# Modulation rows of the first block in two column halves, and part of a later row summed on VectorE

## The reference, cut to what matters

```python
mod = silu_c @ w_ada[l] + b_ada[l]
shift_m, scale_m, gate_m, shift_f, scale_f, gate_f = jnp.split(mod, N_MOD, axis=-1)

h = modulate(rmsnorm(x, g_norm_mix[l]), shift_m, scale_m)   # h * (1 + scale) + shift
proj = h @ w_in[l]
...
x = x + gate_m[:, None, :] * mix
```

## Time and profile before

| | us |
|---|---|
| median of 3 runs | 2786.18 |
| the runs | 2789.58, 2786.18, 2762.64 |
| the profiled execution | 2768.54 |
| its span, first to last instruction | 2766.9 |
| what lies around the span | 1.64 |
| PE busy | 2641.7 (95%) |
| DVE busy | 1923.6 (70%) |
| ACT busy | 1112.8 (40%) |

### The profile page before, as it was taken

One profiled execution on the slowest core, in us unless ns is written; L12 is line 12 of the kernel. 1 busy time (PEld: TensorE's weight loads), 2 busy tenths in 40 slices (PEclk: granted clock), 3 DMA queues, 4 the chain that ended last, 5 costly groups with the idle time before them and its releaser, 6 DMA issues.

```text
span 2766.9 us, 53993 instructions
## 1 busy us (share of the span) xinstructions
PE 2641.7 (95%) x21560; PEld 2477.9 (90%) x21560; DVE 1923.6 (70%) x2016; ACT 1112.8 (40%) x1270; POOL 171.6 (6%) x281
## 2 busy tenths in 40 slices
PE   6999998899999999998998999999979999999998
PEld 2676777799999999997998989999959999999997
DVE  1446576777787776878867888888767466575664
ACT  1334443434343443444333444444434344343443
POOL 5000000100000000100000000001010000000000
PEclk8899999899999999998999999999979999999998
DMA  9997756678888887885766665568737676666753
GB/s 367 345 354 262 218 187 202 197 265 289 278 290 302 285 288 243 298 280 188 246 222 191 220 214 174 164 221 282 270 115 238 204 232 214 204 229 206 230 196 113
DMA packets 301892, 658.80 MB, mean 238 GB/s; under 512 B 30688, under 2 KB 37176, under 8 KB 299320
## 3 DMA queue, kind: packets, MB, share of 16 engines
q1 hardware_dynamic: 269496, 539.35, 57.9%
q0 software_dynamic: 32256, 117.45, 13.1%
HBM read 654.62 MB, written 2.10 MB: 237 GB/s over the span
## 4 chain that ended last, share of the span: by engine, by line
PE 85%; DVE 7%; DMA 3%; ACT 2%; issue 2%; SPq 0%; DVEq 0%; ACTq 0%; POOLq 0%
PE ps L1789 25%; PE ps L1790 24%; PE ps L1791 24%; DVE lo L1008 2%; PE ps L1834 1%; DMA proj<-in_w_ada 1%; PE ps L1836 1%; PE ps L1835 1%; ACT hi L606 1%; PE ps L1995 1%; DVE work L1020 1%; DMA ada_ring<-in_w_ada 1%; PE ps L1948 0%; PE ps L2253 0%; DMA raw<-in_w_in 0%
## 5 line engine op out<-in xcount | busy, mean ns | idle before, releaser
L1008 DVE TENSOR_TENSOR lo<-raw,hi 128x1024 fp32r<-128x1024 f32 x868 | 1049.2, 1222 | 648.5 <-ACT hi L606 646.5
L606 ACT ACTIVATE hi<-raw 128x1024 fp32r<-128x1024 f32 x868 | 911.3, 1059 | 1272.5 <-PE ps L1791 988.6
L1789 PE MATMUL ps<-acts,hi 128*128 128x256 f32 x4432 | 1249.4, 282 | 26.3 <-DVE lo L1008 12.0
L1790 PE MATMUL ps<-acts,hi 128*128 128x256 f32 x4432 | 1236.3, 279 | 0.0
L1791 PE MATMUL ps<-acts,lo 128*128 128x256 f32 x4432 | 1236.1, 279 | 0.0
L1789 PEld LDWEIGHTS ps<-acts,hi 128*128 128x128 f32 x4432 | 841.2, 190 | 67.8 <-issue 46.6
L1790 PEld LDWEIGHTS ps<-acts,hi 128*128 128x128 f32 x4432 | 840.4, 190 | 1.4 <-issue 0.8
L1791 PEld LDWEIGHTS ps<-acts,lo 128*128 128x128 f32 x4432 | 839.3, 189 | 0.4
L1789 PE MATMUL ps<-f_acts,hi 128*128 128x256 f32 x2048 | 566.7, 277 | 0.8 <-DVE lo L1008 0.8
L1790 PE MATMUL ps<-f_acts,hi 128*128 128x256 f32 x2048 | 565.8, 276 | 0.0
L1791 PE MATMUL ps<-f_acts,lo 128*128 128x256 f32 x2048 | 565.8, 276 | 0.0
(11 more groups left out here) (259 smaller groups left out, 1324.3 us busy)
## 6 DMA issues: line engine op xcount, KB each, us to landing
raw<-in_w_ff SPq DMA_DIRECT2D x512, 512.0 KB, 4.7
raw<-in_w_in SPq DMA_DIRECT2D x232, 512.0 KB, 4.6
ada_ring<-in_w_ada POOLq DMA_DIRECT2D x224, 512.0 KB, 5.0
proj<-in_w_ada SPq DMA_DIRECT2D x32, 1024.0 KB, 8.3
proj<-in_w_ada SPq DMA_DIRECT2D x40, 512.0 KB, 5.6
ada_ring<-in_w_ada SPq DMA_DIRECT2D x34, 512.0 KB, 5.9
raw<-in_w_out SPq DMA_DIRECT2D x32, 512.0 KB, 5.0
raw<-in_w_o SPq DMA_DIRECT2D x32, 512.0 KB, 5.2
```

Source lines behind the costliest of these rows:

```text
L606: nc.scalar.activation(hi[n % SPLIT][:, :], raw[n % RAW][:, :], ACT.Copy).then_inc(hi_ready, 1)
L1008: V.tensor_tensor(lo[n % SPLIT][:, :], raw[n % RAW][:, :], hi[n % SPLIT][:, :].bitcast(F32), ALU.subtract)\
L1789: M(out, h, right[:, 0:S], start=start, stop=False)
L1790: M(out, h, right[:, S:2 * S], start=False, stop=False)
```

## The change

Four things are changed.

1. Scale and shift are made in two column halves. Block 0 takes 8 double-row tiles of scale columns 0 to 1023 and 8 of shift columns 0 to 1023; block 1 the same for columns 1024 to 2047, now 16 tiles between chunks 1 and 9 (`tiles_after`). There are four `turn_block` steps in place of three.
2. The first 8 row tiles of segment 2 become 16 halves of 512 KB. DVE multiplies each with its silu column and adds it to one of two accumulators (`ada_halves`), after the split of the chunk that `half_lo` names: twelve behind chunks 16 to 24, four behind chunks 28 to 31. Each is loaded behind the chunk two later than that (`ada_half`). PE adds the accumulators up once, after chunk 31 (`sum_halves`). The other 24 tiles of segments 2 and 3 stay pairs on PE, now after chunks 33 to 62; before, 16 of the 32 stood after chunks 12 to 30. The row of segment 2 is finished one group later.
3. In the last group ahead of a norm DVE writes the output first and splits the next chunk behind it (`out_first`; for the first output projection by its own loop).
4. Pieces of the three big later norms are 1, 1, 2, 4, 4 and 4 tiles, and PE waits for them tile by tile.

The diff, cut to its core:

```diff
-PAIRS, EARLY, LEAD = 3, 2, 3
+PAIRS, LEAD = 3, 3
+HALVES = KT
...
+        half_tiles = pair_tiles[0] + pair_tiles[2]
+        half_landed = [sem(f"half_landed{i}") for i in range(len(half_tiles))]
+        half_used = sem("half_used")
...
-        pair_after = {(PER_BLOCK + 5 * p // 4 if p < KT else FIRST + 12 + 26 * (p - KT) // 15): p for p in range(2 * KT)}
-        tile_after = {j: j - 2 for j in range(2, 10)}
+        half_lo = (16, 17, 18, 19, 19, 20, 21, 21, 22, 23, 23, 24, 28, 29, 30, 31)
+        pair_after = {(33 + 8 * (p - 8) // 7 if p < KT else 43 + 19 * (p - KT) // 15): p for p in range(HALVES // ADA, 2 * KT)}
+        BLOCK_ROWS = 2 * BLOCKS
+        TILES = 2 * KT // BLOCKS
+        tiles_after = {1: (0,), 2: (1, 2), 3: (3,), 4: (4, 5), 5: (6,), 6: (7, 8), 7: (9, 10), 8: (11, 12), 9: (13, 14, 15)}
...
-            return [(0, 2), (2, 4), (4, 8), (8, 12), (12, 16)] if tiles == KT else [(0, tiles)]
+            if tiles < KT:
+                return [(0, tiles)]
+            return [(0, 1), (1, 2), (2, 4), (4, 8), (8, 12), (12, 16)]
...
-            def scale_tile(k):
-
-                start_slot(k, w_ada[0][k * P:(k + 1) * P, D:2 * D].rearrange("(t p) n -> p t n", p=P))
-
-            def shift_tile(b, m):
-
-                rows = w_ada[0][2 * P * m:2 * P * (m + 1), b * 2 * NC:(b + 1) * 2 * NC]
-                start_slot(KT + 8 * b + m, rows.rearrange("(t p) n -> p t n", p=P))
+            def block_tile(b, m):
+
+                col = (m // 8 == 0) * D + b * 2 * NC
+                rows = w_ada[0][2 * P * (m % 8):2 * P * (m % 8 + 1), col:col + 2 * NC]
+                start_slot(TILES * b + m, rows.rearrange("(t p) n -> p t n", p=P))
...
-                if n - LEAD in pair_after and pair_after[n - LEAD] >= EARLY:
+                for h, at in enumerate(half_lo):
+                    if n - 2 == at:
+                        ada_half(h)
+                if n - LEAD in pair_after:
                     ada_pair(pair_after[n - LEAD])
 
+            def ada_half(h):
+
+                k, u, half = h // ADA, h % ADA, D // ADA
+                if 2 <= h < 4:
+                    sp.wait_ge(ada_used, ADA * 2 * KT)
+                if h >= 4:
+                    sp.wait_ge(half_used, h - 3)
+                sp.dma_start(half_tiles[h % 4], w_ada[0][k * P:(k + 1) * P, 2 * D + u * half:2 * D + (u + 1) * half])\
+                    .then_inc(half_landed[h % 4], 16)
...
-                if p >= PAIRS - 1:
+                q = p - HALVES // ADA
+                if q >= PAIRS:
                     sp.wait_ge(ada_used, ADA * (2 * KT + p - PAIRS + 1))
+                elif q == 1:
+                    sp.wait_ge(ada_used, ADA * (2 * KT + HALVES // ADA))
+                else:
+                    sp.wait_ge(half_used, HALVES)
...
-            for k in range(KT):
-                scale_tile(k)
-            for m in range(8):
-                shift_tile(0, m)
+            for m in range(TILES):
+                block_tile(0, m)
             for j in range(PER_BLOCK):
                 start_chunk(j)
-                for m in {3: (0,), 4: (1, 2), 5: (3,), 6: (4, 5), 7: (6,), 8: (7,)}.get(j, ()):
-                    shift_tile(1, m)
-            for p in range(EARLY):
-                ada_pair(p)
+                if j == 3:
+                    for m in range(START):
+                        block_tile(1, m)
+                for m in tiles_after.get(j - 3, ()):
+                    if m + START < TILES:
+                        block_tile(1, m + START)
             for j in range(PER_BLOCK):
                 start_chunk(PER_BLOCK + j)
...
-                    split_chunk(n + c + SPLIT, d)
+                    if not (out_first and c == per - 1):
+                        split_chunk(n + c + SPLIT, d)
 
                     for h in range(c * halves // per, (c + 1) * halves // per):
                         ada(h % ADA, *adas[h // ADA])
@@ -1052,6 +1079,8 @@
 
                 dve.wait_ge(weights_used, n + per + d)
                 out(out_banks(g, tiles))
+                if out_first:
+                    split_chunk(n + per - 1 + SPLIT, d)
...
-                finish_block(b + 1)
+                finish_block(2 * b + 1)
                 for c in range(4):
                     split_chunk(n0 + c)
                     block_low(b, c)
                 for j in range(4, PER_BLOCK):
                     split_chunk(n0 + j)
-                    if b == 0 and j == 7:
+                    ada_halves(n0 + j)
+                    if b == 0 and j == 10:
+                        finish_block(2)
                         block_normed(1)
             split_chunk(FIRST)
+            ada_halves(FIRST)
             for g in range(OPEN):
                 split_chunk(FIRST + g + 1)
                 dve.wait_ge(weights_used, FIRST - OPEN + g + 1)
                 plain(proj[:, DQ + 4 * g:DQ + 4 * g + 4, :])(ps[:, 2 * g:2 * g + 2, :].rearrange("p b (j n) -> p (b j) n", n=S))
...
             dve.wait_ge(sin_ready, 1)
+
+            def rope_and_halves(c):
+
+                ada_halves(FIRST + SPLIT + c)
+                if c % 3 == 0:
+                    g = c // 3
+                    rope(proj[:, DQ + 4 * g:DQ + 4 * g + 4, :], cos_d, sin_d)
+
             group(FIRST, OPEN, out=plain(proj[:, DQ + 4 * OPEN:DQ + 4 * OPEN + 4, :]),
-                  after={3 * g: lambda g=g: rope(proj[:, DQ + 4 * g:DQ + 4 * g + 4, :], cos_d, sin_d) for g in range(OPEN)})
+                  after={c: lambda c=c: rope_and_halves(c) for c in range(FULL)})
...
-                    group(n0 + FULL * (g1 + q), g0 + g1 + q, adas=adas(q), out=out(q), after=after(q))
+                    group(n0 + FULL * (g1 + q), g0 + g1 + q, adas=adas(q), out=out(q), after=after(q), out_first=q == 3)
...
-                    if fresh and CK * c in fresh:
-
-                        pe.wait_ge(*fresh[CK * c])
-
                     pe.wait_ge(lo_ready, n + c + 1 + d)
                     h = hi[slot][:, 0:CK * width].rearrange("p (t n) -> p t n", n=width)
                     l = lo[slot][:, 0:CK * width].rearrange("p (t n) -> p t n", n=width)
                     for t in range(CK):
                         k = CK * c + t
+                        if fresh and k in fresh:
+                            pe.wait_ge(*fresh[k])
...
             for j in range(PER_BLOCK):
                 start_chunk(j)
-                if j in tile_after:
-                    shift_tile(1, tile_after[j])
+                for m in tiles_after.get(j, ()):
+                    block_tile(1, m)
+                if j == 7:
+                    turn_block(2)
                 if j == PER_BLOCK - 2:
-                    turn_block(2)
+                    turn_block(3)
             for n in range(PER_BLOCK, FIRST):
                 start_chunk(n)
                 if n in pair_after:
                     pair(pair_after[n])
...
+            def sum_halves():
+
+                pe.wait_ge(half_used, HALVES)
+                pe.wait_ge(mods_block, BLOCK_ROWS)
+                for j in range(4):
+                    last = M(ps[32 * j:32 * j + 32, 6, :], ones[:, 0:32], work[:, j // 2, (j % 2) * NC:(j % 2 + 1) * NC], start=True, stop=False)
+                last.then_inc(ada_used, HALVES)
+
             group(FIRST, OPEN, pairs=True,
                   after={3 * g: lambda g=g: turn("turn_diff", proj[:, DQ + 4 * g:DQ + 4 * g + 4, :], OPEN - 1) for g in range(OPEN)})
+            sum_halves()
...
+            def ada_halves(n):
+
+                for h, at in enumerate(half_lo):
+                    if at == n:
+                        u = h % ADA
+                        tile, col, part = half_tiles[h % 4], silu[:, h // ADA:h // ADA + 1], work[:, u, :]
+                        dve.wait_ge(half_landed[h % 4], 16 * (h // 4 + 1))
+                        if h < ADA:
+                            V.tensor_scalar(part, tile, col, None, ALU.mult).then_inc(half_used, 1)
+                        else:
+                            dve.wait_ge(half_used, h - 1)
+                            V.scalar_tensor_tensor(part, tile, col, part, ALU.mult, ALU.add).then_inc(half_used, 1)
+
...
-                split_chunk(n0 + p + SPLIT)
+                if p < len(OUT1) - 1:
+                    split_chunk(n0 + p + SPLIT)
...
+            split_chunk(n0 + len(OUT1) - 1 + SPLIT)
```

100 lines of the change are left out of this document (43 added, 57 removed).

## The result

Ten runs of the changed kernel have a median of 2796.4 us (2771.0 to 2806.8), ten of the kernel before beside them 2771.5 (2762.6 to 2790.9). The ratio is 1.0067, 95% interval 1.0039 to 1.0096: slower by 0.4 to 1.0% (the two medians alone give 1.0090). Forecast was 2760, range 2735 to 2782. The profiled run of the kernel after took 2806.8 us (span 2805.1), the longest of its ten.

The account below looks back on a forecast made before the run. PE, busy for 95% of the span, was taken as the bound, with loads setting the start. Opening -10.6 and norms -6.3 make -16.9 us: 2751.6 on the profiled execution, 2760 from the runs' mean 2776.7; range 2735 to 2782.

Parts of the forecast that it names:

- The prediction's own sign of being wrong: The prediction is wrong if time moves between 600 and 1080 us, where the change has nothing.
- The slower step stays: Rival, chance 0.05: PE's matmul stream keeps its 3% slower rate through one or both feed-forwards; +14 us, 2791.
- The opening, -10.6 forecast: Start of the kernel: tiles, turn, load wait, pairs, halves' sum and chunk 24 wait total -10.6 us, bounds -20 and -4.
- -20.5 for the eight tiles: Opening: eight tiles less ahead of the first chunk, 2.56 us each, -20.5 us.
- +13.0 up to chunk 12: Opening: eight tiles more between chunks 1 and 9, +9.8 us, one more turn, +1.7, and a load wait, +1.5.
- The load wait of 1.5: Opening: PE and the loads reach block 1's last tile together at 114.4 us; wait 0 to 4.5, +1.5 taken.
- The wait ahead of chunk 24: Opening: PE waits for DVE's second copy, late behind the halves; +5.5 us, 0 to 7.5.
- -9.8 and +1.2 for the pairs: Opening: eight pairs fewer on PE, -9.8 us, and `sum_halves`, the same four matmuls, +1.2.
- The norms, -6.3: Later norms: -5.7 us for the split behind the output and -0.6 for the smaller first piece.
- The split behind the output: Three later norms: the split leaves the chain, 2.3, 1.14 and 2.3 us, -5.7 in all.
- The wait ahead of the second block's first projection: Norm without idle waits: a first piece of one tile lets PE start earlier, 1.2 us at most, -0.6 taken.
- The zero of the smaller piece: Ahead of both feed-forwards: PE comes no earlier by the one-tile piece because it passes 64 and 128 idle waits; 0 us.

Follow-up runs that it names:

- e3_fit: The changed kernel with 70 idle waits more on PE at the norm ahead of the second feed-forward, moving its loop by 36 instructions; median 2757.6 us.
- e11_blocks: The changed kernel with the opening in two blocks but no halves on DVE, all 32 tiles as pairs on PE; median 2761.2 us.
- e2_norms: The kernel before with only the three edits of the later norms; median 2765.8 us, ratio to before 0.993 to 0.999.
- e6_waits: The changed kernel with the feed-forwards' idle waits moved to where PE waits anyway, plus as many more as e3_fit has; median 2755.5 us.

## Why the prediction was wrong

**The step that failed.** The sum put at nothing all that happens to PE's stream behind the opening and the norms. Two things happened there. Of the 38.2 us between the two spans (2805.1 and 2766.9) the slower step makes some 34, two stops 11.2 and the low clock behind them 3.7; what is left for the forecast's own terms is some -11 where -16.9 stood, of which the rows named below hold 8.6. The prediction's own sign of being wrong came true: from the start of the first feed-forward to its end the kernel after takes 15 us longer, where the change has nothing. The profile of the kernel after is its longest run; between the medians, 24.9 us apart, the step would be some 21 by the same subtraction, which is not measured.

**The slower step was on the list, and underrated.** It is the other-side rival, "The slower step stays": it gave 2791 and got 0.05. What it named happened, the slower step in both feed-forwards. What I wrote against it, that the trace left it by itself at 640 us, was one draw taken for a habit. In the 19 profiles here the first feed-forward's loops began at the slower step eight times: in 5 of the 14 with the new opening and in 3 of the 5 without it.

**Not in the prediction at all: the instruction stream.** A loop on PE that no longer fits where it lies cost 11.2 us of stops and 3.7 us of cold clock (granted clock 0.58 from 2235 to 2240 us and 0.69 from 2417 to 2422), 14.9 together, and 16.3 by the lowest runs of after and e3_fit. The rows were there: the idle waits ahead of both feed-forwards do nothing but move what follows, and I read them only as time. A change that takes 49 instructions off PE ahead of a loop, by my count, had to be checked for that. The Trainium skill, Runtime: NRT & Kernel Launch, section "Instruction fetch mechanics", says that PE's instruction memory holds 2048 instructions as a queue filled in blocks of 256, and that a taken branch to a target outside the current window of two such pages waits for its load. This trace agrees in the packets of 16 KB and in the stops. It does not agree in the window of two: the first feed-forward's loops of the kernel before take six packets from 550 to 680 us and none from 700 to 1070, though they branch back in between. The page gives no price, the rows do: 5.3 to 6.1 us and the clock.

**The opening, -10.6 forecast, -1.3 at chunk 56.** -20.5 for the eight tiles: -19.4, right. +13.0 up to chunk 12 (9.8, 1.7 and 1.5): +18.1. The load wait of 1.5 was 1.5, but the turn behind it waited 1.9 for ACT, and a low clock followed: 0.82, 0.50 and 0.83 in the three stretches of 6 us from 102 on are 5.1 us below full speed, part of it while PE waited. The sum had no term for these two. The wait ahead of chunk 24, 5.5 forecast and 7.5 at worst: 7.2, right, with 1.7 us of cold clock behind it (0.29 of the 6 us from 174 on) that I had left out. By the rate that the Trainium skill has in DMA: Bandwidth & Descriptors, section "Anatomy of one DMA — SWDGE (gpsimd) path", an estimate which I weighed against the rows, it would have been 2.7; the page's rate is for DMAs that GpSimd issues, SP issues these, and the rows were the better guide. -9.8 and +1.2 for the pairs were not measured by themselves; with that wait and its clock, +8.9, they make about 0, as chunks 12 to 56 show (1.3 us ahead at both). With e11_blocks the whole splits into nothing for the blocks and nothing for the halves.

**The norms, -6.3: right.** The split behind the output: PE's wait behind the first output projection fell in e2_norms from 5.19 to 2.91 us (-2.3), behind the first feed-forward 5.62 to 3.98 (-1.6, forecast -1.1), behind the second block 4.68 to 2.40 (-2.3). The wait ahead of the second block's first projection, 1.53 us "<-issue" before, is 0.39 in the kernel after (-1.1, forecast -0.6). The zero of the smaller piece ahead of the two feed-forwards was right for the kernel as it stands; e6_waits shows that 4.9 us were hidden behind the idle waits.

**The sum.** With the loop put back (e3_fit) the ratio is 0.9925 to 0.999 and the median 2757.6, against 2760 forecast (2751.6, and 8.4 from the profiled execution to the runs). That is not a hit: the lowest runs differ by 8 us (2754.7 against 2762.6), and the rest of the medians' 17 would be the draw of the step. In the profiles, with the slower step's time taken off both spans, e3_fit is 14 us under before (2736 and 2750), of which about 9 stand in the waits and starts named here. Of the rest, 3.5 are no work of the change: e3_fit, whose program up to there is that of the kernel after, starts the first feed-forward at 538.2 and not 541.7, with a granted clock of 0.96 and 0.97 from 310 to 350 and from 350 to 400 us, where the kernels after and before both had 0.91 and 0.93. Less than 2 us are unexplained.

**Open.** What sets the step. Seen is: it changed at breaks (the rise of the clock, a stop, matmuls of another shape), held at least until the next, differed between runs of one program, and repeated at one place of a loop. Its cause is not known, and no kernel here holds it at the faster one; so whether the changed kernel as it stands meets the slower step more often than the one before is not shown either.

## To carry to other kernels

When PE's instruction count ahead of a loop changes, look at the instruction packets and at the first matmul behind each branch back before anything else; idle waits can move the loop to where it fits, and they belong where PE waits anyway. A gain made at the start is only kept if what was hidden under the waits has other cover: here eight tiles, a turn, short waits and their cold clock took back 18 of 19 us. Where a kernel's runs fall into two heaps, compare lowest runs and step counts by stretch as well as medians, and price a rival by how long a known state may last, not by how long it lasted once.
